# Transposes of the identity at TensorE's waits, and four waits changed, in a two-block transformer kernel

## The reference

```
h   = rms_norm(x, g_mix) @ w_in                       # -> u_f, u_q, u_kv, u_kr
x   = x + concat(fourier_mix(u_f), mla_attention(u_q, u_kv, u_kr)) @ w_out
x   = x + memory_cross_attention(rms_norm(x), rms_norm(mem))     # 256 memory rows, 4 heads of 256
x   = x + expert_choice_moe(rms_norm(x))              # 16 experts, top 128 tokens each, 1024 wide
x   = rms_norm(x, g_final)
# second block
h   = rms_norm(x) * (1 + scale) + shift               # scale, shift, gate = c @ w_ada + b_ada
glu_a, glu_b, z_conv, q, k, v, z_att, g_conv, g_att = split(h @ w_in_2)
u      = silu(layer_norm(causal_conv31(glu_a * sigmoid(glu_b))))
y_conv = (u * silu(z_conv)) @ w_conv_out
att    = windowed attention of 3 x 8 heads, dilations 1, 4, 16, merged by softmax weight
y_att  = (att * silu(z_att)) @ w_att_out
x      = x + gate * ((sigmoid(g_conv) * y_conv + sigmoid(g_att) * y_att) @ w_o)
out    = rms_norm(x)
```

## Time and profile before

| what | value |
|---|---|
| time, 3 runs | 2930.61 us median (2928.8 to 2931.55) |
| the profiled execution's own time | 2932.97 us |
| its span, first to last instruction | 2931.2 us |
| mean granted TensorE clock | 0.978 |
| busy: PE, weight load, VectorE, ScalarE, GpSimd | 96%, 79%, 61%, 43%, 16% |
| experts, 1000 to 1500 us | PE busy 500 of 500 us at clock 1.00, DMA 393 GB/s |
| instructions | 35949 |

### The profile page before, as it was taken

One profiled execution on the slowest core, in us unless ns is written; L12 is line 12 of the kernel. 1 busy time (PEld: TensorE's weight loads), 2 busy tenths in 40 slices (PEclk: granted clock), 3 DMA queues, 4 the chain that ended last, 5 costly groups with the idle time before them and its releaser, 6 DMA issues.

```text
span 2931.2 us, 35949 instructions
## 1 busy us (share of the span) xinstructions
PE 2801.9 (96%) x14268; PEld 2306.2 (79%) x14268; DVE 1782.0 (61%) x2498; ACT 1245.8 (43%) x2011; POOL 459.5 (16%) x423
## 2 busy tenths in 40 slices
PE   8999999999998999999995999999999999999998
PEld 6978888867884688888874887878878868588888
DVE  4645888322435788888875777777677764110564
ACT  4224787232210677777766124454443342011101
POOL 1400231000000211111104000000001063132241
PEclk9999999999998999999996999999999999999999
DMA  4130000411215999999974121030211212010131
GB/s 137 47 138 15 30 1 9 168 68 65 72 44 190 361 389 393 393 397 397 397 269 144 58 92 53 19 112 26 79 46 32 96 58 72 16 56 29 51 137 58
DMA packets 141459, 382.27 MB, mean 130 GB/s; under 512 B 11743, under 2 KB 45025, under 8 KB 141164
## 3 DMA queue, kind: packets, MB, share of 16 engines
q1 hardware_dynamic: 125036, 324.17, 29.3%
q0 software_dynamic: 13520, 46.28, 5.0%
q10 hardware_dynamic: 2736, 9.50, 0.9%
HBM read 340.47 MB, written 39.46 MB: 130 GB/s over the span
## 4 chain that ended last, share of the span: by engine, by line
PE 71%; DVE 6%; ACT 2%; issue 1%; DMA 1%; POOL 0%; SPq 0%; POOLq 0%; ACTq 0%; DVEq 0%
PE ps L2722 7%; PE ps L2723 7%; PE ps L2724 7%; PE ps L2707 6%; PE ps L2709 6%; PE ps L2708 6%; PE ps L2369 5%; PE ps L2355 4%; PE ps L2781 2%; PE ps L2783 2%; PE ps L2782 2%; PE ps L2824 2%; PE ps L2793 2%; PE ps L2795 2%; PE ps L2794 2%
## 5 line engine op out<-in xcount | busy, mean ns | idle before, releaser
L2135 DVE SCALAR_TENSOR_TENSOR b_f<-b_f,small_f 128x1023 f32<-128x1023 f32 (+14 forms) x240 | 304.3, 1268 | 69.6 <-ACT small_f L1219 40.9
L2722 PE MATMUL ps<-x_f32r,w_f32r 128*128 128x512 f32 x480 | 188.3, 392 | 0.8 <-issue 0.8
L2724 PE MATMUL ps<-x_f32r,w_f32r 128*128 128x512 f32 x480 | 187.1, 390 | 0.0
L2708 PE MATMUL ps<-w_f32r,a_f32r 128*128 128x512 f32 x456 | 178.0, 390 | 0.0
L2723 PE MATMUL ps<-ht_f32r,w_f32r 128*128 128x512 f32 x416 | 162.1, 390 | 0.0
L2782 PE MATMUL ps<-w_f32r,a_f32r 128*128 128x512 f32 x384 | 150.7, 392 | 0.0
L2722 PE MATMUL ps<-ht_f32r,w_f32r 128*128 128x512 f32 x320 | 126.9, 397 | 9.4 <-issue 4.8
L2355 PE MATMUL ps<-small_f 128*128 128x128 f32 (+1 forms) x696 | 100.0, 282 | 36.6 <-DVE small_f L1760 26.3
L2724 PE MATMUL ps<-ht_f32r,w_f32r 128*128 128x512 f32 x320 | 126.0, 394 | 0.0
L2708 PE MATMUL ps<-x_f32r,a_f32r 128*128 128x512 f32 x312 | 122.6, 393 | 0.0
L2355 PEld LDWEIGHTS ps<-small_f 128*128 128x128 f32 (+1 forms) x696 | 82.6, 142 | 45.3 <-DVE small_f L1760 28.1
(11 more groups left out here) (496 smaller groups left out, 7883.2 us busy)
## 6 DMA issues: line engine op xcount, KB each, us to landing
w_f<-in_w_exp_up SPq DMA_DIRECT2D x40, 1024.0 KB, 10.0
w_f<-in_w_exp_down SPq DMA_DIRECT2D x38, 1024.0 KB, 8.3
w_f<-in_w_exp_gate SPq DMA_DIRECT2D x36, 1024.0 KB, 8.7
x_f<-in_w_exp_gate SPq DMA_DIRECT2D x28, 1024.0 KB, 8.2
x_f<-in_w_exp_down SPq DMA_DIRECT2D x26, 1024.0 KB, 10.3
x_f<-in_w_exp_up SPq DMA_DIRECT2D x24, 1024.0 KB, 10.3
w_f<-in_w_in SPq DMA_DIRECT2D x22, 1024.0 KB, 5.1
w_f<-in_w_in SPq DMA_DIRECT2D x10, 2048.0 KB, 8.1
```

The source lines that it names most:

```text
L2135: ins = v.scalar_tensor_tensor(C_conv[k][:, d:S], U_conv[k][:, 0:S - d], cols[:, k, R_TAP + j:R_TAP + j + 1], C_conv[k][:, d:S], ALU.mult, ...
L2708: mm(o, x1, w2[:, k, c], start=False, stop=False)
L2722: mm(o, l1, r1, start=(k == 0), stop=False)
L2724: ins = mm(o, l2, r1, start=False, stop=(k == n - 1))
```

## The change

A function `spare_turns(name, n)` begins the bank of a product that comes later and turns the identity into it n times; nobody reads the result, and the product overwrites it. It is called in front of waits of TensorE. The first conditional below stands in a loop or in a branch each time, so that the turns are made at fifteen points of a run.

The last tile of the memory attention gets a second pair of rounded rows (in the place of two probability buffers), and its `om` is moved ahead of tile 6's product; `square` and `scale` of the last tile are moved ahead of `n3` and `lg` of tile 6. The first `mk` product waits for each half of `mnT` on its own. The copies that make the first dilated step's parts are moved up, each behind the reads that free its place, and VectorE's sum for `HT` behind them. The output product waits for 31 merged blocks at tile 0 and for 32 at tile 4.

```diff
@@ att2_steps
                 if t == T - 1:
-                    steps = [("square", t - 2), ("scale", t - 2), ("pt", t), ("om", t - 1), ("pv", t), ("n3", t - 2), ("lg", t - 2), ("y", t - 1)]
+                    steps = [("square", t - 2), ("scale", t - 2), ("pt", t), ("om", t - 1), ("pv", t), ("n3", t - 2), ("lg", t - 2), ("om", t), ("y", t - 1)]
                 elif t == T:
-                    steps = [("square", t - 2), ("scale", t - 2), ("om", t - 1), ("y", t - 1), ("n3", t - 2), ("lg", t - 2)]
+                    steps = [("square", t - 2), ("scale", t - 2), ("y", t - 1), ("square", t - 1), ("n3", t - 2), ("scale", t - 1), ("lg", t - 2)]
+                elif t == T + 1:
+                    steps = [("n3", t - 2), ("lg", t - 2)]
@@ ScalarE and VectorE, memory attention
-        omt_hi, omt_lo = (mem_r(GB0 + 2048 + 1024 * i, 1024).rearrange("p (k s) -> p k s", k=KC) for i in range(2))
+        omt = [[mem_r(at_, 1024).rearrange("p (k s) -> p k s", k=KC) for at_ in pair] for pair in ((GB0 + 2048, GB0 + 3072), (GC0, GC0 + 2048))]
+        def omt_parts(t):
+            return omt[t == T - 1]
-                    if t >= 1:
+                    if t == T - 1:
+                        bk.wait(act, ("p2", t - 1, 1)), bk.wait(act, ("o2", t - 1, 1))
+                    elif t >= 1:
                         bk.wait(act, ("ym", t - 1, 1))
-            bk.wait(act, ("o2", T - 1, 0)), bk.wait(act, ("o2", T - 1, 1))
+            bk.wait(act, ("ym", T - 1, 1))
@@ ScalarE, behind split_hi("k") of the last gate products
+                    bk.read(act, ("glu_a", 3, 1, 0))
+                    nc.scalar.activation(tile_parts[0][0], value(group_tokens(*tiles2[0], src=HT_r)), ACT.Copy).then_inc(sem("tile_hi"), 1)
...
             chunk_out(6, U[6])
             bk.read(act, ("glu_a", 3, 1, 1))
-            nc.scalar.activation(tile_parts[0][0], value(group_tokens(*tiles2[0], src=HT_r)), ACT.Copy).then_inc(sem("tile_hi"), 1)
-            bk.read(act, ("glu_a", 3, 1, 0))
@@ VectorE
                         split_lo("qk"[pos // 2], GORDER[0])
+                        if pos == 2:
+                            v.tensor_copy(tile_parts[0][1], value(group_tokens(*tiles2[0], src=HT_Xr))).then_inc(sem("tile_lo"), 1)
...
-            bk.read(dve, ("glu_a", 3, 1, 1))
-            v.tensor_copy(tile_parts[0][1], value(group_tokens(*tiles2[0], src=HT_Xr))).then_inc(sem("tile_lo"), 1)
+            bk.wait(dve, ("glu_a", 3, 1, 1))
             dve.wait_ge(sem("tile_hi"), 1)
+            dve.wait_ge(sem("tile_lo"), 1)
@@ TensorE
+            def spare_turns(name, n):
+                b = bk.begin(pe, name)
+                for _ in range(n):
+                    turn(PS[:, b, 0:P], ident)
...
+                if t == 0:
+                    spare_turns(("uf", 0), 24)
                 u_product(("uf", t), 0, t, NB)
...
+                        if t == 0:
+                            spare_turns(("s1", 0), 8)
                         pe.wait_ge(sem("block1_lo"), 6 + t // 4)
...
-                if c == 0:
-                    for m in range(2):
-                        bk.read(pe, ("nm", m, 0)), bk.read(pe, ("nm", m, 1))
+                for k in range(KC):
+                    if c == 0 and k % 4 == 0:
+                        bk.read(pe, ("nm", 0, k // 4)), bk.read(pe, ("nm", 1, k // 4))
...
                 if i == 5:
+                    spare_turns(("idx",), 26)
                     pe.wait_ge(sem("top"), 1)
...
+                    if x == 0:
+                        spare_turns(("xT", 0, 0), 8)
                     pe.wait_ge(sem(f"xg_in{x % 2}"), 16 * (x // 2 + 1))
...
                         bk.begin(pe, (m, e, j))
+                    if (m, e) in (("g", 0), ("d", NE - 1)):
+                        spare_turns((m, e, 0), 12)
...
                 if i == 0:
+                    if c == 0 and nm == "b":
+                        spare_turns((f"glu_{nm}", i, c, h), 30)
                     pe.wait_ge(sem("n4_split"), T + T * h)
...
+                if t == 0:
+                    pe.wait_ge(sem("x_tile0"), XB_IN)
+                if t < T // 2:
+                    spare_turns(("n4", t, 0), 38 if t == 0 else 12)
                 pe.wait_ge(sem("n4b_hn"), t + 1)
...
                 elif kind == "v":
+                    if t == 0 and i > 0:
+                        spare_turns(("wv", g, t), 20)
...
                         bk.read(pe, ("c1", t - 1, j))
+                    if t == 2:
+                        spare_turns(("c2", 1, 0), 24)
                     for j in range(2):
                         turns(("c2", t - 1, j), HN[(t - 1) % 2][:, NB * j:NB * j + NB])
...
-                    if j == 0 and t == 0:
-                        pe.wait_ge(sem("tmp_used"), 32)
+                    if j == 0 and t % 4 == 0:
+                        pe.wait_ge(sem("tmp_used"), 31 + t // 4)
```

More of the change, by code:

```diff
@@ L1439, in _ @@
                         b = bk.wait(act, ("om", t, j))
-                        nc.scalar.activation(omt_hi[:, 4 * j:4 * j + 4, :], b4(b), ACT.Copy).then_inc(sem("psum_hi"), 1)
+                        nc.scalar.activation(omt_parts(t)[0][:, 4 * j:4 * j + 4, :], b4(b), ACT.Copy).then_inc(sem("psum_hi"), 1)
                 elif kind == "square":
@@ L1991, in _ @@
                         b = bk.at[("om", t, j)][0]
-                        k4 = slice(4 * j, 4 * j + 4)
-                        bk.done(v.tensor_tensor(omt_lo[:, k4, :], b4(b), value(omt_hi[:, k4, :]), ALU.subtract), ("om", t, j))
+                        hi, lo = (x[:, 4 * j:4 * j + 4, :] for x in omt_parts(t))
+                        bk.done(v.tensor_tensor(lo, b4(b), value(hi), ALU.subtract), ("om", t, j))
                 elif kind == "pv":
@@ L2564, in _ @@
             for c in range(8):
-                if c == 0:
-                    for m in range(2):
-                        bk.read(pe, ("nm", m, 0)), bk.read(pe, ("nm", m, 1))
                 if c % 4 == 0:
                     w_wait(pe, f"mkv{c // 4}")
-                product(("mk", c), lambda k: wview(f"mkv{c // 4}")[:, k, tile(c % 4)], lambda k: mnT[:, k, :], KC, lambda b: PS[:, b, 0:MEM])
+                b = bk.begin(pe, ("mk", c))
+                for k in range(KC):
+                    if c == 0 and k % 4 == 0:
+                        bk.read(pe, ("nm", 0, k // 4)), bk.read(pe, ("nm", 1, k // 4))
+                    ins = mm(PS[:, b, 0:MEM], wview(f"mkv{c // 4}")[:, k, tile(c % 4)], mnT[:, k, :], start=(k == 0), stop=(k == KC - 1))
+                bk.end(ins, ("mk", c))
                 pe.wait_ge(sem("norm_hn"), HNORM["n2"] + c + 1)
@@ L2624, in _ @@
                     bk.read(pe, ("om", t, 0)), bk.read(pe, ("om", t, 1))
+                    omt_hi, omt_lo = omt_parts(t)
                     for j in range(2):
```

## The result

The changed kernel takes 2903.76 us (median of 4 runs, 2901.25 to 2907.79), the kernel before 2929.70 beside it: ratio 0.991, 95% interval 0.9895 to 0.9925, so 25.9 us less (the forecast was 21.6 less and 2909.0). Timed again later it took 2905.53 against 2931.01 (ratio 0.9915, 0.9902 to 0.9929). The profiled execution took 2902.55 us, span 2900.7, granted clock 0.992 instead of 0.978.

A forecast was written before the change was run, and what follows sets the result against it. TensorE's own work, its waits and the half clock behind them were taken as the bound. Terms -11.0 - 4.6 - 5.0 - 0.6 - 1.5 - 2.8 + 3.3 + 0.6 = -21.6 us off 2930.61 gave 2909.0, range 2900 to 2919.

The forecast's parts named there:

- the likeliest case: The forecast itself: turns hold the clock and the other terms add up, 2909.0 us, its own range 2903 to 2914, chance 0.62.
- the stretch at 891.8: Half-clock stretch caused by the memory tail's wait; it goes with that wait, 1.6 us of the 11.0 clock gain.
- the turns on the path: Turns not hidden: 30 before the second half's gate product, +3.3 us, and 8 before the first score product, +0.6.
- memory tail: Memory attention's end: last tile's wait goes, -4.6 us; square and scaling before tile 6's router result, -5.0.
- Rival 1: Turns don't hold the clock: the 11.0 us shrink to 1.6, total 2918 us; chance 0.10.
- The routing group: Groups of 26, 8 and 12 turns around routing and the first expert's gather, priced at nothing.
- rival 4: Slower: the bank ends last at most places, so 288 turns (31.4 us) stand on the path, 2946 us; chance 0.04.
- rival 3: The 30 turns at 1606.18 are hidden after all and first experts run at full clock: 2902 to 2906 us; chance 0.10.
- Gain 3.8 to 6.3; -5.0: Memory tail's new order: last add to last turns falls from 15.4 us to 11.6 or some 9.1; taken as -5.0.
- the prediction's sign: Sign of being right in the memory tail: last turns some 10 us after the last add.
- rival 2: The memory tail's gain does not reach the expert stage, since stores and gather end last: 2919 us; chance 0.12.
- the dilated term: First dilated parts: some 2 us of a 2.9 us wait go, mostly becoming a later weight-load wait; -1.5, bounds 0 and 4.5.

The follow-up runs named there:

- no_turns: The changed kernel with the 288 turns left out, everything else kept: 2912.68 us, ratio 0.9938 to the kernel before.
- turns_only: The kernel before with the fifteen groups of turns and none of the other edits: 2924.04 us, ratio 0.9975 to the kernel before.
- small_undone: The changed kernel with the waits at key product, dilated parts and output product as before: 2913.71 us, ratio 0.9939 to the kernel before.
- after_again: The changed kernel timed again with no edit: 2905.53 us, ratio 0.9915 to the kernel before.
- more_turns: The changed kernel with the second half's thirty turns in free bank 4 and three more groups of turns: 2897.20 us, ratio 0.9887 to the kernel before.
- real_products: The changed kernel with each of the 288 turns made an ordinary product of the identity with itself: 2918.47 us, ratio 0.9956 to the kernel before.

## Why the prediction was right, point by point

The time lay in the range, 5.2 us below the point, and the mechanism of the likeliest case held. That the sum came so near is in part luck: the tail was forecast 1.5 us too high and the other terms 3.8 to 5.3 too low. The terms, put together as the runs can tell them apart:

| part | forecast | shown |
|---|---|---|
| turns: clock without the stretch at 891.8, less the turns on the path (-9.4 + 3.9) | -5.5 | -7.2 (no_turns), -7.5 (turns_only) |
| memory tail with that stretch (-4.6 - 5.0 - 1.6) | -11.2 | -9.7 by the two traces |
| key product, dilated parts, output product (-0.6 - 1.5 - 2.8) | -4.9 | -7.0 to -8.2 (small_undone) |
| sum | -21.6 | -23.9 to -25.4; measured -25.9 and -25.5 |

No run undoes the last tile's own rounded rows alone, so -9.7 rests on the traces. It fits the times: no_turns stands 18.3 us below the kernel before, where tail and small waits make 16.7 to 17.9.

**The turns hold the clock.** This was the step for which no row of before spoke. The first product, the last down product, the first gate product, the two later groups' values and the layer norm are six places where turns fill a wait. The two traces without turns, before and no_turns, have a stretch at half clock in 11 of 12 of them; the eleven traces with turns or their like in 3 of 66, all three at the second dilation group's values, where 2.0 us of the wait are left behind the turns. Where turns start late or waits stay behind them (the gathered tokens, the second half's gate product) the clock still fell. The Trainium skill (TensorE: Matmul & The Clock Gate, Part 4: PE-mode transpose) says that transposes don't count as busy for the clock in the same way; by that rule no_turns would have been no slower, and it was 7.2 slower. Real products of the same length did no better. Rival 1 falls: turns hold the clock. They raise it too, and not only in the trace of before: in the trace after, behind the wait for the reloaded tile TensorE did nothing but turns, the first sixteen at clock 0.50 (1525.98 to 1529.39), and from 1531.5 on the clock was 1.00.

```profile
1525.98 9.50 PE L2365 MATMUL ps<-small_f 128*128 128x128 f32 x58 [11.58 <-DMA b_f<-acc]
```

**The turns on the path.** The thirty at 1582.93 had the sigmoid as releaser, as forecast. They took 4.7 us, and the product behind them won 2.7 back at full clock against before and 1.6 against no_turns: 2.0 and 3.1 net; forecast 3.3. In the trace of after_again they took 5.9, so one trace gives this to 1.2 us only. The eight at the score product delayed the first one by 0.9 us and the third, whose wait shrank from 1.79 to 1.37 us, by 0.5 (forecast 0.6). The bank is late nowhere else, so rival 4 had no place beyond the one read, and rival 3 fell there.

**The routing group and the reloaded tile.** Priced at nothing, and no more than that can be told from the traces. From the last turns of the tail to the first expert it is 57.75 us before, 56.6 in no_turns, and 56.6 to 58.0 in the six traces with the same groups of turns. From the last down product to the first gate product it is 50.5 us in no_turns and 49.5 to 50.6 in those six (51.1 before, where the down product was at half clock).

**The tail.** The last tile's wait of 4.58 us went whole. From the first router product of the tail (871.97 before, 864.09 after) to the last add the gain is 6.4 us: 4.6 for the wait and 1.8 for the clock behind it. The rest of the tail is the step that failed: "Gain 3.8 to 6.3; -5.0". The order gave 3.3 (12.0 us from the last add to the last turns, where the prediction's sign was some 10). Its two parts to the last tile's turns came as forecast (4.2 us from add to turns), but the wait of 2.06 us ahead of the last router product left that product at half clock (3.56 us), the lower end of the forecast's own two; and VectorE's copies started at 896.34, behind the softmax steps of tile 6 that now stood ahead of them. The forecast took the middle of a range when the row of before showed this very product at half clock behind a shorter wait. more_turns filled that wait and took the 1.6 us. All 17.6 us of the affinities' lead reached the first expert, so rival 2 falls: the gather's DMA was issued earlier with the indices.

**The three small waits.** The second step that failed. The key product: "the fourth of VectorE's copies ... one is 0.6" took the copies to go tile by tile. The code writes both memory tiles' first halves before the second halves, so TensorE waits for two copies less, not one: its wait went from 2.94 to 1.53 us, 1.4 less where 0.6 was forecast. And the forecast counted the half clock behind the dilated parts, but at neither of the other two. Behind the key product it was in plain sight in the trace of before (564.0 to 567.4); behind the output product it was absent there, by chance, as turns_only and small_undone show. The output product's own 2.8 was right (3.0), and so was the dilated term, limited by the weight's DMA (1.5 forecast, 1.6 shown).

What stays open is why a wait of 1.2 to 2.1 us sometimes costs half clock and sometimes not. Each of the thirteen traces has such a stretch behind one or two of the waits at 290, 508, 710 and 866, and not the same ones. It is some 1.7 us each, which may be part of the changed kernel's spread of 6.5 us.

## What to carry to other kernels

A wait of TensorE costs its own length and, behind it, some 1.7 us more when the clock falls; price both, even where the one trace at hand shows no fall of the clock. Dummy turns in a bank pay if they start when the wait starts, so choose a bank that is already empty, not the bank of the product that they stand in front of: here the same thirty turns cost 3.9 us more in the bank of the next product than in an empty one. When a chain of small steps on three engines is shortened, look at whether its last TensorE step still meets half clock, since that may be a third of the gain.

## What the runs showed of the hardware

An ordinary float32 product of 128x128 by 128x128 is recorded as two matmuls, each of a turn's length, so it takes twice the time of a transpose of the same size: twelve at full clock 2.84 us in real_products against 1.47, thirty, partly at half clock, 9.2 against 4.7. And the same wait of 2.8 us at the output product left the clock at 1.00 in the trace of before and at 0.50 in two others, so one trace does not tell what a wait costs in clock.
